# Order of the matmuls within a weight piece: all with the high weights first, then all with the low weights

## The reference

```python
for i in range(DEPTH):                       # DEPTH = 2
    u = rmsnorm(h, norm_mix_g[i])
    h = h + (rglru_mixer(u, ...) if i % 2 == 0 else ssd_mixer(u, ...))
    h = h + swiglu(rmsnorm(h, norm_ffn_g[i]), ffn_w_gate[i], ffn_w_up[i], ffn_w_down[i])
    gate = sigmoid(rmsnorm(h, norm_ple_g[i]) @ ple_w_gate[i])
    h = h + gate * (p[i] @ ple_w_proj[i])
return rmsnorm(h, final_norm_g)
```

## Time and profile before

| what | value |
|---|---|
| median of the 3 runs | 2766.11 us |
| lowest, highest run | 2753.71, 2769.26 us |
| the profiled execution, its own time | 2769.57 us |
| its span in the trace | 2767.8 us |
| mean granted TensorE clock | 0.993 |
| busy: TensorE matmul, weight load | 98%, 89% of the span |
| busy: VectorE, ScalarE, GpSimd | 73%, 48%, 14% |
| DMA | 502 MB, 181 GB/s |

### The profile page before, as it was taken

The page is one execution under the profiler, slowest core; times in us unless marked ns, Lnnn a source line. Parts: engine busy times, 40 slices in busy tenths (PEclk is TensorE's granted clock), DMA queues, the critical chain, the costliest instruction groups (busy, mean ns, idle before and its releaser), DMA issues.

```text
span 2767.8 us, 51496 instructions
## 1 busy us (share of the span) xinstructions
PE 2708.5 (98%) x17871; PEld 2464.4 (89%) x17871; DVE 2031.0 (73%) x2802; ACT 1342.2 (48%) x1818; POOL 382.6 (14%) x418
## 2 busy tenths in 40 slices
PE   7999999999999999999999999999999999999997
PEld 7998888888888888999998999988888888888897
DVE  8887876665666677888886788878666556666776
ACT  5665344444444444456664566634444444444443
POOL 3333200000000121201110011121000000001122
PEclk9999999999999999999999999999999999999999
DMA  5555566656656665555555655556555666565554
GB/s 194 185 180 157 177 197 189 190 175 191 203 190 189 191 191 163 188 169 178 173 178 167 198 172 173 179 157 197 182 186 179 178 201 185 187 187 171 184 178 149
DMA packets 158369, 502.35 MB, mean 181 GB/s; under 512 B 17792, under 2 KB 20160, under 8 KB 157120
## 3 DMA queue, kind: packets, MB, share of 16 engines
q1 hardware_dynamic: 158192, 501.04, 58.1%
q10 hardware_dynamic: 80, 0.07, 0.0%
HBM read 498.88 MB, written 2.16 MB: 181 GB/s over the span
## 4 chain that ended last, share of the span: by engine, by line
PE 83%; DVE 9%; issue 4%; ACT 3%; POOL 1%; DMA 0%; DVEq 0%; ACTq 0%; SPq 0%; POOLq 0%
PE bank L381 42%; PE bank L383 21%; PE bank L364 6%; PE bank L366 6%; PE bank L365 6%; DVE wlo L821 3%; DVE arena L973 2%; ACT whi L575 1%; DVE R L878 0%; DVE arena L975 0%; PE bank L540 0%; DVE arena L1201 0%; PE bank L544 0%; ACT arena L755 0%; PE bank L542 0%
## 5 line engine op out<-in xcount | busy, mean ns | idle before, releaser
L381 PE MATMUL bank<-R,whi 128*128 128x512 f32 x4992 | 1754.5, 397 | 12.0 <-POOL R L1323 6.1
L821 DVE TENSOR_TENSOR wlo<-wraw,whi 128x1024 fp32r<-128x1024 f32 (+3 forms) x1056 | 1208.4, 1155 | 575.6 <-ACT whi L575 572.7
L575 ACT ACTIVATE whi<-wraw 128x1024 fp32r<-128x1024 f32 (+3 forms) x1056 | 993.2, 947 | 955.8 <-PE bank L383 767.1
L383 PE MATMUL bank<-R,wlo 128*128 128x256 f32 x4992 | 1395.2, 279 | 0.0
L381 PEld LDWEIGHTS bank<-R,whi 128*128 128x128 f32 x4992 | 939.5, 188 | 240.3 <-POOL R L1323 8.4
L383 PEld LDWEIGHTS bank<-R,wlo 128*128 128x128 f32 x4992 | 943.2, 189 | 0.1
L364 PE MATMUL bank<-R,whi 128*128 128x256 f32 x2368 | 683.6, 289 | 21.6 <-DVE R L878 13.0
L365 PE MATMUL bank<-R,whi 128*128 128x256 f32 x2368 | 673.0, 284 | 0.0
L366 PE MATMUL bank<-R,wlo 128*128 128x256 f32 x2368 | 672.9, 284 | 0.0
L364 PEld LDWEIGHTS bank<-R,whi 128*128 128x128 f32 x2368 | 456.7, 193 | 30.2 <-issue 15.5
L365 PEld LDWEIGHTS bank<-R,whi 128*128 128x128 f32 x2368 | 457.6, 193 | 2.2 <-issue 1.9
(11 more groups left out here) (165 smaller groups left out, 1365.7 us busy)
## 6 DMA issues: line engine op xcount, KB each, us to landing
wraw<-in_F SPq DMA_DIRECT2D x352, 512.0 KB, 3.9
wraw<-in_B SPq DMA_DIRECT2D x224, 512.0 KB, 3.6
wraw<-in_A SPq DMA_DIRECT2D x96, 512.0 KB, 3.8
wraw<-in_F SPq DMA_DIRECT2D x128, 384.0 KB, 3.1
wraw<-in_F SPq DMA_DIRECT2D x128, 320.0 KB, 3.2
wraw<-in_PL SPq DMA_DIRECT2D x64, 320.0 KB, 3.2
wraw<-in_PL SPq DMA_DIRECT2D x64, 256.0 KB, 2.8
arena<-cs_rows SPq DMA_DIRECT2D x8, 1024.0 KB, 5.8
```

Source lines behind the costliest of these rows:

```text
L381: nc.tensor.matmul(dst.rearrange("p (s t) -> p s t", s=2), whi[:, q % RING, cols], src[:, :, k, :], start=first, stop=False)
L383: mm = nc.tensor.matmul(dst[:, 0:SEQ], wlo[:, q % RING, cols], src[:, 0, k, :], start=False, stop=last)
L575: nc.scalar.activation(whi[:, slot, 0:w * BLOCK], wraw[:, slot, 0:w * BLOCK], ACT.Copy).then_inc(w_hi, 1)
L821: V.tensor_tensor(wlo[:, slot, 0:w * BLOCK], wraw[:, slot, 0:w * BLOCK], whi[:, slot, 0:w * BLOCK].bitcast(F32), ALU.subtract).then_inc(w_ ...
```

## The change

Within a piece TensorE now issues first, for every block, the matmuls with the high weights, after a wait for `w_hi` alone; then it waits for `w_lo` and issues, for every block, the matmul with the low weights. The waits of single blocks (`before`) stay with the high matmuls. `w_used` is still raised by the last matmul with low weights. Number and shape of the matmuls are unchanged, and the rest of the program too.

```diff
                 p = it * len(ph["widths"]) + ph["piece0"] + q
-                pe.wait_ge(w_lo, p + 1)
+                pe.wait_ge(w_hi, p + 1)
                 for b, (before, dst, src, k, first, last) in enumerate(blocks):
                     for s, v in before:
                         pe.wait_ge(s, v)
                     cols = slice(b * BLOCK, (b + 1) * BLOCK)
-                    if ph["name"] not in WIDE:
-                        mm = three(dst[:, 0:SEQ], whi[:, q % RING, cols], wlo[:, q % RING, cols], src[:, 0, k, :],
-                                   src[:, 1, k, :], first, last)
-                        continue
-
-                    nc.tensor.matmul(dst.rearrange("p (s t) -> p s t", s=2), whi[:, q % RING, cols], src[:, :, k, :],
-                                     start=first, stop=False)
+                    if ph["name"] in WIDE:
+                        nc.tensor.matmul(dst.rearrange("p (s t) -> p s t", s=2), whi[:, q % RING, cols], src[:, :, k, :],
+                                         start=first, stop=False)
+                    else:
+                        nc.tensor.matmul(dst[:, 0:SEQ], whi[:, q % RING, cols], src[:, 0, k, :], start=first, stop=False)
+                        nc.tensor.matmul(dst[:, 0:SEQ], whi[:, q % RING, cols], src[:, 1, k, :], start=False, stop=False)
+                pe.wait_ge(w_lo, p + 1)
+                for b, (before, dst, src, k, first, last) in enumerate(blocks):
+                    cols = slice(b * BLOCK, (b + 1) * BLOCK)
                     mm = nc.tensor.matmul(dst[:, 0:SEQ], wlo[:, q % RING, cols], src[:, 0, k, :], start=False, stop=last)
                 mm.then_inc(w_used, 1)
```

## The result

The changed kernel takes 2774.32 us in the median of 15 runs (2772.72 to 2775.73); the kernel before, run beside it, 2766.11 us (2751.40 to 2781.67, 15 runs). The ratio is 1.0045, with a 95% interval of 1.0025 to 1.0065: slower, by less than the 0.5% that was set as the bound of no change. Forecast were 2769 us, a range of 2744 to 2796 us, and "within 0.5%" as the likeliest.

The account below looks back on a forecast made before the run. TensorE was taken as the bound, matmuls busy 98% of the span. The terms -4 + 0 + 0 - 2 + 5 = -1 us against the profiled 2769.6 us gave 2769 us, range 2744 to 2796 us.

Parts of the forecast that it names:

- step 3: Wide phases: a block goes from 0.3499 to 0.3491 us, over 4992 blocks, -4 us.
- the hidden load: Rival, wide phases: weight load stops showing, high matmuls in runs reach 0.2135 us, -92 us, 2681 us; chance 0.06.
- The slow rhythm: Rival, wide phases: high matmuls in runs take 0.2355 us, block 0.3535 us, 2791 to 2800 us; chance 0.24.
- The fixed cost: Rival, wide phases: each matmul costs its columns plus 0.0133 us, high runs 0.2268 us, 2747 us; chance 0.22.
- Step 4: Phases other than the wide ones: every 256-column matmul stays at 0.120 us, 0 us.
- Step 5: Middle of each of 1056 pieces: the added semaphore wait is covered by the running matmul, 0 us.
- Step 6: Low-weight waits in PL and before B1: starting high matmuls early gains 2 us (bounds 0 and -6.6 us).
- Step 7: A1, A2, B2: low matmuls now stand behind the last late operand, +5 us (bounds +2 to +7 us).
- all-quick run: Wide phases before the change: all blocks in the quick rhythm would save 17 us, giving 2753 us.

Follow-up runs that it names:

- 9: Changed kernel put back to alternation, except a settling piece in new order early in A2, B2, F1, then a high-high-low-low pair; 2754.34 us, ratio 0.9975.
- 10: As 9, with the same settling pieces but without the pairs: 2785.58 us, ratio 1.0095.
- experiment 2: Changed kernel, new order kept, but `w_lo` waited for at the head of each piece: 2774.02 us, ratio 1.0036.
- kernel 3: Changed kernel with the old order in pieces whose tiles come late (fifth of A2 and B2, first two of A1): 2768.54 us, ratio 1.0015.
- kernel 1: Changed kernel with the old block-by-block order, keeping `w_hi` at the head and `w_lo` before the first low matmul: 2757.43 us, ratio 0.998.
- kernel 8: Changed kernel put back to the old order, except the last two blocks of each piece as high, high, low, low: 2768.32 us, ratio 1.0033.
- kernel 7: Changed kernel put back to the old order, except the first two blocks of each piece as high, high, low, low: 2767.90 us, ratio 1.0043.

## Why the prediction was right

**What bounds, and step 3.** The forecast rested on the mean block staying as it was: 0.3491 us. The counts give 0.3491 and 0.3490 us in all, and the phases 0.3492 us in F1 and 0.3503 us in F2, whose shorter runs the forecast did not treat apart. This is why the term was mis-sized: of the -4 us, 3.4 us belong to the 4224 blocks of F1 and F2, and these won 7.4 - 6.5 = 0.9 us. Of its two terms, the 512 behind a 512 was put at 0.2311 and is 0.230 us, the 256 behind a 256 at 0.118 and is 0.119 us. The rivals on that term: the hidden load (0.2135 us) is out. The slow rhythm, as the rival put it (0.2355 us in the high runs, block 0.3535 us), is out; but it was right that the slow rhythm is what costs most in this kernel, and that such a thing is the difference between kernels of the same matmuls, 31 us between kernels 9 and 10. The fixed cost is half right: the intervals late in a run, 0.226 to 0.227 us (in the expectation for runs of four), are its 0.2268 us, and its block of 0.3467 us is the quick alternation; but the first intervals of a run are longer, and runs of eight never reach it in the mean.

**Step 4** held: the second B1 half, 640 blocks without a wait that differs, takes 1805.92 - 1545.37 = 260.55 us before and 1815.64 - 1555.07 = 260.57 us after.

**Step 5**, the added wait at 0 us, held: kernels with one and with two waits in a piece differ by 0.3 us and have the same count of blocks in a window to one in 2048 (2).

**Step 6**, the early start, was put at -2 us and is within 1 us of nothing. The waits shrank as forecast (6.6 to 1.5 + 0.6 us, with the 3.3 us at the head of B1 reassigned), but order alone, with the full wait at the head of the piece, is as fast. PL of layer 0 does gain 1.5 us. The next wait, that of B1's first block for its bank, gives back the little by which it grew, from 3.35 to 3.7 us; the rest went in the profiled run with the fall of the clock at 1220 us, shown under experiment 2.

**Step 7**, the late operands, was put at +5 us and measured as 5.8 us (3), as a sum. Of its single terms that of A2 can be read in the timeline after, that of A1 can't. A2 against the earlier trace rows:

```profile
256.01 0.79 PE L377 MATMUL bank<-R,whi 128*128 128x512 f32 x1 [0.93 <-POOL R L1280]
256.61 1.91 PE L385 MATMUL bank<-R,wlo 128*128 128x256 f32 x8
258.31 1.91 PE L377 MATMUL bank<-R,whi 128*128 128x512 f32 x4
```

The eight lows behind the last tile take 258.31 - 256.61 = 1.70 us at half clock, and the next piece begins 3.7 us later than before, 2.4 us of which A2 brought along from A1: +1.4 us, against 1.3 forecast. A1 against the earlier trace rows:

```profile
25.87 0.41 PE L381 MATMUL bank<-R,whi 128*128 128x256 f32 x1
26.09 1.91 PE L385 MATMUL bank<-R,wlo 128*128 128x256 f32 x8
27.79 0.41 PE L380 MATMUL bank<-R,whi 128*128 128x256 f32 x1
```

Here the next piece begins at 27.79 instead of 25.92, +1.9 us, above the 1.7 us of the upper bound: the matmuls of 256 columns are still 0.21 us apart, where before they were 0.12 us apart at this time. (The row of the granted clock says 1.00 in both kernels here; the intervals are those of half clock.) The order isn't shown to be the cause. The 0.12 us begin at 25.7 us in before, at 29.2 us in the changed kernel, but also at 29.7 us in kernel 1 and at 28.9 us in kernel 3, which have the old order in these pieces. Kernel 1 begins its third piece at 26.16 us and still A2 at 235.02 us, 1.7 us later than before; kernel 8, also in the old order but for the pairs, begins A2 at 233.09 us. So most of A1's 2.4 us is a difference that kernels of the old order have among themselves. In B2 the first half lost the 1.4 us forecast, the second 2.4 us, with a granted clock of 0.80 from 1825 to 1842 us, against 0.90 in the 17 us around its late tiles before (1815 to 1832 us).

**What went past the forecast** was the yardstick. It compared with one profiled execution of 2769.6 us and took the halves of the earlier trace rows for what every execution has. It did see that an all-quick run would be the lowest of the three runs, but not that the rhythm is drawn once a layer and so makes groups, nor that the new order ends the draw. Against the lowest group of before, the changed kernel loses about 19 us (0.7%), against the middle one about 5. So that the medians lay within 0.5% of each other, as forecast, was luck of the mix. The absolute time is no luck of this kind, since the 0.349 us doesn't depend on the draw, but it was missed by 5 us, and that between the two profiled executions as well (+4.4 us where -1 us was forecast): the blocks of F1 and F2 won 2.5 us less than their share of the forecast, the early start brought nothing where 2 us were put down, and the late operands cost 1 us more.

## What to carry to other kernels

Where TensorE is busy throughout and the same matmuls run thousands of times, the interval from start to start is the quantity to know, to a nanosecond, and counting one line in two long windows gives it; an earlier start of work that is nearly always waiting for the engine gave nothing here. Where the runs of a kernel lie in groups, look in a profile of each group for what differs before any change is judged by medians. And when work is split into a part that needs a late operand and a part that doesn't, keep the second as filling between arrivals: put behind the last one, it costs its whole length.

## What the runs showed of the hardware

A strict alternation of a 512-column and a 256-column fp32r matmul, each with its own weight load, has two stable rhythms at full clock, 0.3466 and 0.3533 us a block of one each. It keeps either for over 700 us, through loops, phases and other shapes of pieces. It changed at a float32 product in between (at 338.82 us above), and, in B2 of kernel 1, across a wait for late tiles and the half clock behind it (slow up to 1476 us, quick from 1484 us). A pair of each kind within the alternation swaps the two (41 and 41 pieces in turn in kernel 7, and in 8). Which one it takes can be set by what comes right before: behind 256-column matmuls settled at 0.120 us straight alternation gave the slow one (10, all 6 runs at 2783.8 us and above), with a pair first the quick one (9, all 12 runs at 2758.5 us and below). Behind such matmuls that ran mostly at half clock it was the other way round (A2 of both). Runs of two, four and eight of a kind have one rhythm each, 0.3484, 0.3507 and 0.3491 us, and none of them reaches the quick alternation's 0.3466 us. At half clock there is no such excess: 0.43 and 0.21 us are 1.2 columns per ns.

Why the alternation has two rhythms, and what the excess of some 13 ns a matmul over half of its interval at half clock (0.120 against 0.107 us) is, no run here settles. Runs longer than eight weren't tried.
